# Softmax weights of the mixers scaled on ScalarE instead of VectorE, and tile 0's expert rows placed 3.45 apart in the written order of a one-core decoder layer

## The chip, the cores and the metric

One core of a Trainium2 chip runs the whole program. The metric is device time in microseconds (us), the median of three runs. TensorE is called PE below, VectorE DVE, ScalarE ACT, GpSimd POOL and SyncE SP, as the profile does. Everything is fp32, except where a projection splits its operands into a high and a low part.

## The reference, cut to what matters

1024 new prompt tokens and 64 sample tokens pass one decoder layer. Two mixers (a gated recurrence, "GLA", and windowed attention with a sink) read one input projection; their gated sum goes through an output projection; then a retrieval layer ("PEER") picks 128 of 16384 one-neuron experts for each token. The attention weights are what the change touches:

```
s = q . k * HD**-0.5, masked;  m = max(max_k s, sink)
e = exp(s - m);  p = e / (sum_k e + exp(sink - m));  o = p @ v        # 16 heads, 256 keys
```

and the expert layer is what fills most of the time:

```
act = gelu(x . u[idx_k]);  out = sum_k g_k * act_k * v[idx_k]         # k = 0..127 for each token
```

Each u row and v row is 4 KB. One gather brings one expert row for each of the 128 tokens of a tile, so 128 u gathers and 128 v gathers for a tile, 0.5 MB each.

## The kernel before, in words

Tokens come in 8 prompt tiles of 128 (0 to 7) and a tile of 64 sample tokens (8). The work before the experts goes in phases: projection of tiles 0 to 2, mixer of tile 0, feed group 0 (merge of the two branches, output projection, norm, queries and key scores for the experts of tile 0); then mixers of tiles 1 and 2 and feed group 1; then the projection of tiles 3 to 5, mixers 3 to 5 and feed group 2; then the projection of tiles 6 to 8, mixers 6 and 7, the samples' mixer and feed group 3. The expert layer of the tiles already scored runs beside this, and alone at the end.

The order of each engine's instructions is written out by a planner. Every piece of work is a generator (`mix_dve`, `mix_act`, `mix_pe`, `expert_dve`, ...) that yields the *place* of its next piece, a number of about a microsecond; `merged` takes, for each engine, always the piece with the smallest place. A place is no time: once the order is written, each engine runs its list strictly in order, and a piece waits for its semaphores with all that stands behind it. POOL has a list of its own without places: for each tile and head the u gathers, and from tile 1 on after each u gather one v gather of the tile before. The ring of u rows (L1881) holds 8 gathers, freed by the dot products, the ring of v rows (L1891) holds 8, freed by PE's sums.

Experts count in *slots*, one u row of one tile in each. Slot p has the place

```
at_slot(p) = start + p * SLOT_US + gaps at or before p
```

On DVE a slot is one dot product of 128 x 1024 (L2096) and, in 13 of a head's 16 slots, one step of the selection of the experts two heads ahead (L1970 to L2025). On PE the sums of tile t (L2180) stand from slot 128 (t + 1) on, the first one 5 slots later. On ACT, the gelu of tile t (L1923) stands at slot 128 (t + 1) + 0.2, followed by the copies that PE's sums need (L1926, L1935). A gap is put in so that the selection of a tile's first head does not stand ahead of its scores: slot 96 is at least 8 behind the scores of feed group 1, slot 352 at least 8 behind those of group 2.

The places that matter, worked out from the code (planner numbers, not measured times): `start` 393.6; mixer 1 from 423.1 and mixer 2 from 507.1 to 591.1; feed group 1 from 595.1 to 784.1 (its scores of head 1 at 732.1); slot 96 at 740.1 and slot 128 at 832.9; the projection of tiles 3 to 5 from 790.4 to 1037.4, its first product at 803.0; mixers 3 to 5 from 1045.4 to 1297.4; slot 352 at 1496.8.

Inside the mixer of tile t (`mix(t, x)`, x in steps of 1.05 places, for tile 0 1.3): DVE takes the attention scores from PSUM (L1173), ACT does the 16 exponentials with their sums (L1043) and `e_done`; the four recurrence heads go on beside it. Recurrence head h needs exponents (DVE, L1104), their exponentials (ACT, `gla_exp`, L1019 to L1022), `rescale` (DVE, L1114), scores (PE, L1234), `masked` (DVE, L1126), the output (PE, L1243, L1244), the copy `kpT` (ACT, L1049), the state update (PE, L1253) and `advance` (DVE, L1131). After x = 64 PE turns the scaled attention weights (L1293), ACT copies them (L1060), PE multiplies by the values (L1304). DVE's scaling stands at x = 48 to 51, between the exponents of head 3 and `masked` of head 2.

Of the kernel before, what the change touches and what calls it, by code (L numbers as in the profile page):

```python
# [23 lines left out]
ALU = mybir.AluOpType  # L24
ACT = mybir.ActivationFunctionType
AX_X = mybir.AxisListType.X

P = 128
# [14 lines left out]
SWA_HEADS, KV_HEADS, HD, WINDOW = 16, 2, 64, 128  # L43
# [124 lines left out]
MIX_PHASES = ((0,), (1, 2), (3, 4, 5), (6, 7))  # L168
FEEDS = len(FEED_TILES)
KEPT = FEEDS - 1  # L170
SLOT_US = 2.90
MIX_US = 80.0
SAMPLE_US = 150.0
KEYS = WINDOW + STEPS
# [5 lines left out]
def layer_stage(nc, sem, i_, o_, z_tok, z_feat, z_kv, z_kT, z_b, oa_rows, ob_cols, h_rows, xn_rows, scores):  # L180
# [6 lines left out]
    with ExitStack() as ctx:  # L187
# [148 lines left out]
        M, N_ = shared(mix_fill), shared(sample_fill)  # L336
# [47 lines left out]
        s_taken = sem("m_s_taken")  # L384
        neg_ready = sem("m_neg_ready")
        e_done = sem("m_e_done")
        p_ready = sem("m_p_ready")
        pT_ps = sem("m_pT_ps")
        pT_ready = sem("m_pT_ready")
# [141 lines left out]
        def mix(t, x):  # L531
            base, stretch = mix_at[t]
            return base + stretch * x
# [8 lines left out]
        start = scored(0, 1) + 26.0  # L542
        gaps = []

        def at_slot(p):
            return start + p * SLOT_US + sum(extra for first, extra in gaps if p >= first)

        for g in range(1, FEEDS):
            first = (FEED_TILES[g][0] * HEADS - 2) * TOPK
# [485 lines left out]
        def mix_act(act, t):  # L1035
# [9 lines left out]
            for h in range(GLA_HEADS):  # L1045
                yield mix(t, (34.5, 42.3, 53.5, 60.0)[h])
                act.wait_ge(sc_done, GLA_HEADS * t + h + 1)
                wait(act, su_done, GLA_HEADS * t + h - 1)
                act.activation(M.kpT[:, h % 2, :], X[:, BANK + h * P:BANK + (h + 1) * P], ACT.Copy).then_inc(kpT_ready, 1)  # L1049
                if h < 2:  # L1050
                    yield mix(t, exp_at(h + 2))
                    gla_exp(act, t, h + 2)
            yield mix(t, 62.5)
            norm_squares(act, M, t, P)
            yield mix(t, 65.0)
# [100 lines left out]
        def mix_dve(dve, chain, t):  # L1156
# [43 lines left out]
            yield mix(t, 48.0)  # L1200
            dve.wait_ge(e_done, t + 1)
            chain.link(dve.tensor_tensor(M.m[:, 3, :], M.e_sum[:, :], M.m[:, 2, :], ALU.add))
            chain.link(dve.reciprocal(M.m[:, 3, :], M.m[:, 3, :]))
            for q in range(4):
                if q:
                    yield mix(t, 48.0 + q)
                heads = slice(4 * q, 4 * q + 4)
                last = dve.tensor_tensor(M.s[:, heads, :], M.s[:, heads, :],
                                         M.m[:, 3, heads].unsqueeze(2).to_broadcast([P, 4, 2 * P]), ALU.mult)
                if q < 3:  # L1210
                    chain.step(last)
            last.then_inc(p_ready, 1)
            yield mix(t, 52.5)
            masked(dve, t, 2)
            yield mix(t, 53.5)
# [1084 lines left out]
```

## Time and profile before

| | |
|---|---|
| median of 3 runs | 4101.09 us (4090.44 to 4101.35) |
| the profiled execution | 4111.9 us, its span 4110.1 us |
| PE busy | 3062.5 us (75%) |
| DVE busy | 2435.0 us (59%) |
| POOL busy | 2350.9 us (57%) |
| ACT busy | 715.2 us (17%) |
| moved by DMA | 1450.92 MB, mean 353 GB/s |

Busy shares are means over stages with different limits; the stages have to be read one by one. "DMA share" is the mean busy share of the core's 16 DMA engines; it reads up to 1.03 or 1.04 where they are full.

### The profile page before, as it was taken

How to read it: one execution, taken by the hardware profiler on the slowest of the kernel's cores; microseconds unless marked ns; L12 is line 12 of the kernel's file. 1: busy time of each engine (PE TensorE's matmuls, PEld its weight loads, DVE VectorE, ACT ScalarE, POOL GpSimd, SP SyncE). 2: the span in 40 equal slices, each digit the busy share in tenths (PEclk: the TensorE clock that was granted, in tenths of full speed). 3: DMA queues.
4: the chain of work that ended last, by engine and by line, in shares of the span. 5: the costliest groups of instructions: out<-in, count | busy, mean ns of one | idle time of the engine just before them, and what ended most of it. 6: DMA issues, size and time to landing. Idle time of an engine off the chain costs nothing.

```text
span 4110.1 us, 40041 instructions
## 1 busy us (share of the span) xinstructions
PE 3062.5 (75%) x14004; PEld 1684.9 (41%) x14004; DVE 2435.0 (59%) x6237; ACT 715.2 (17%) x1573; POOL 2350.9 (57%) x2188
## 2 busy tenths in 40 slices
PE   8988458789957698979876767597965665665667
PEld 7887337677723345547753312244510000010111
DVE  3342885476677855467658857365566666665540
ACT  5461220243223200133222101000100000000000
POOL 0000332255667856466657757566677777777775
PEclk9999559899977799989987766798977777778999
DMA  4537768799999999899999999999999999999999
GB/s 151 165 121 279 252 227 299 243 345 414 413 337 349 344 409 411 334 393 410 414 395 347 366 357 393 380 368 412 412 401 409 409 409 407 409 407 373 397 409 351
DMA packets 451617, 1450.92 MB, mean 353 GB/s; under 512 B 52184, under 2 KB 135192, under 8 KB 431048
## 3 DMA queue, kind: packets, MB, share of 16 engines
q0 software_dynamic: 313344, 1140.99, 71.6%
q1 hardware_dynamic: 138072, 307.37, 20.6%
q8 instruction: 111, 1.82, 0.2%
q14 instruction: 90, 0.74, 0.0%
HBM read 1384.54 MB, written 64.82 MB: 353 GB/s over the span
## 4 chain that ended last, share of the span: by engine, by line
PE 33%; DMA 23%; POOL 21%; issue 10%; DVE 9%; ACT 2%; SPq 1%; POOLq 0%; DVEq 0%; ACTq 0%; PEldq 0%
DMA e_v_rows<-in_v,e_expT 16%; POOL e_v_rows L1891 11%; POOL e_u_rows L1881 10%; PE e_o_ps L2180 7%; PE O L1789 6%; PE X L1754 5%; DVE e_u_rows L2096 3%; PE X L1771 2%; PE e_o_ps L856 1%; PE e_o_ps L858 1%; PE e_o_ps L857 1%; PE X L856 1%; PE U L1805 1%; DMA f_obT<-ob_cols 1%; DMA f_ring<-in_w_feed 1%
## 5 line engine op out<-in xcount | busy, mean ns | idle before, releaser
L1881 POOL DMA_INDIRECT e_u_rows<-in_u,e_expert x1024 | 1119.4, 1093 | 1164.2 <-DVE e_dots L2096 511.8
L2180 PE MATMUL e_o_ps<-e_v_rows,e_zw 128*32 128x512 f32 x4352 | 1236.1, 760 | 580.1 <-DMA e_v_rows<-in_v,e_expT 567.9
L2096 DVE CUSTOM_DVE_ANT_0 e_u_rows<-e_u_rows,e_xn 128x1024 f32<-128x1024 f32 x1088 | 1326.1, 1220 | 533.6 <-DMA e_u_rows<-in_u,e_expert 408.4
L1891 POOL DMA_INDIRECT e_v_rows<-in_v,e_expT x1088 | 1166.9, 1073 | 558.1 <-issue 280.7
L2180 PEld LDWEIGHTS e_o_ps<-e_v_rows,e_zw 128*32 128x32 f32 x4352 | 205.5, 123 | 1481.6 <-DMA e_v_rows<-in_v,e_expT 1143.9
L1789 PE MATMUL O<-f_oaT,f_ring 128*128 128x384 f32 (+2 forms) x1024 | 264.7, 414 | 1.5 <-ACT f_oaT L1646 0.8
L810 DVE TENSOR_TENSOR jb_wl<-jb_w,jb_wh 128x512 fp32r<-128x512 f32 (+1 forms) x200 | 131.9, 688 | 183.6 <-ACT jb_wh L733 183.3
L1789 PEld LDWEIGHTS O<-f_oaT,f_ring 128*128 128x128 f32 x1024 | 176.2, 195 | 79.2 <-issue 13.1
L1754 PE MATMUL X<-f_oaT,f_ring 128*128 128x384 f32 (+2 forms) x512 | 138.8, 427 | 46.8 <-DMA f_ring<-in_w_feed 40.1
L733 ACT ACTIVATE jb_wh<-jb_w 128x512 fp32r<-128x512 f32 (+1 forms) x200 | 120.2, 628 | 156.1 <-PE X L858 77.0
L1754 PE MATMUL X<-f_obT,f_ring 128*128 128x384 f32 (+2 forms) x512 | 135.1, 419 | 15.3 <-DMA f_obT<-ob_cols 15.3
L1771 PE MATMUL X<-f_ring,f_mT 128*128 128x256 f32 x576 | 131.4, 386 | 7.9 <-DVE f_obT L1703 3.5
L856 PE MATMUL X<-jb_xh,jb_wh 128*128 128x384 f32 x360 | 127.0, 353 | 11.2 <-DVE jb_wl L810 11.0
L1754 PEld LDWEIGHTS X<-f_oaT,f_ring 128*128 128x128 f32 x512 | 90.5, 201 | 96.7 <-DMA f_ring<-in_w_feed 41.5
L1935 ACT ACTIVATE e_zw<-e_wT 128x32 f32<-128x32 f32 (+1 forms) x36 | 8.8, 249 | 696.8 <-PE e_o_ps L2180 696.5
L810 DVE TENSOR_TENSOR ja_wl<-ja_w,ja_wh 128x512 fp32r<-128x512 f32 (+1 forms) x100 | 67.4, 691 | 105.0 <-ACT ja_wh L733 104.7
L1771 PEld LDWEIGHTS X<-f_ring,f_mT 128*128 128x128 f32 x576 | 108.8, 192 | 36.0 <-issue 21.9
L857 PE MATMUL X<-jb_xl,jb_wh 128*128 128x384 f32 x360 | 122.5, 340 | 0.0
L858 PE MATMUL X<-jb_xh,jb_wl 128*128 128x384 f32 x360 | 122.4, 340 | 0.0
L1754 PEld LDWEIGHTS X<-f_obT,f_ring 128*128 128x128 f32 x512 | 89.9, 197 | 60.3 <-DMA f_obT<-ob_cols 16.2
L1234 PE MATMUL X<-qt,rel 128*128 128x16 f32 x512 | 90.7, 324 | 28.8 <-DVE kp L1121 28.8
L1234 PEld LDWEIGHTS X<-qt,rel 128*128 128x128 f32 x512 | 92.5, 274 | 41.3 <-issue 35.5
(315 smaller groups left out, 4527.6 us busy)
## 6 DMA issues: line engine op xcount, KB each, us to landing
f_ring<-in_w_feed SPq DMA_DIRECT2D x80, 1024.0 KB, 8.2
jb_w<-in_w_big SPq DMA_DIRECT2D x48, 1024.0 KB, 8.3
ja_w<-in_w_big SPq DMA_DIRECT2D x24, 1024.0 KB, 5.1
e_v_rows<-in_v,e_expT POOLq DMA_INDIRECT x1088, 9.9
e_u_rows<-in_u,e_expert POOLq DMA_INDIRECT x1024, 10.1
z_feat<-jb_stage SPq DMA_DIRECT2D x64, 192.0 KB, 7.6
e_sc<-scores SPq DMA_DIRECT2D x36, 256.0 KB, 6.9
z_feat<-ja_stage SPq DMA_DIRECT2D x32, 192.0 KB, 1.9
```

The lines of the kernel that those rows point to most:

```text
L810: dve.tensor_tensor(quarter(r.wl[q % 2], c, part), quarter(r.w[q % 2], c, part), quarter(r.wh, c, part).bitcast(F32), ALU.subtract).then_i ...
L856: pe.matmul(out, lhs[0][:, k, :], rhs[0][:, k, :], start=(k == 0), stop=False)
L857: pe.matmul(out, lhs[0][:, k, :], rhs[1][:, k, :], start=False, stop=False)
L858: last = pe.matmul(out, lhs[1][:, k, :], rhs[0][:, k, :], start=False, stop=(k == KT - 1))
L1234: pe.matmul(X[:, h * P + j * SUB:h * P + (j + 1) * SUB], M.rel[:, h % 2, j, :], M.qt[:, h % 2, j * SUB:(j + 1) * SUB], start=True, stop=True)
L1754: last = pe.matmul(w_ps[b][:, 0:size(g) * P], weight[:, k, :], src[:, k, 0:size(g) * P], start=(k == 0), stop=(k == KT - 1))
L1771: last = pe.matmul(w_ps[item % 2][:, 0:WIDTH], F.mT[:, k, i * P:(i + 1) * P], weight[:, k, :], start=(k == 0), stop=(k == KT - 1))
L1789: last = pe.matmul(q_ps[half][:, 0:size(g) * P], weight[:, k, half * P:(half + 1) * P], F.xnT[:, k, 0:size(g) * P], start=(k == 0), stop=( ...
L1881: pool.indirect_dma_start(u_ring[:, count % U_RING, :], None, u_dram, bass.IndirectOffsetOnAxis(ap=index, axis=0)).then_inc(u_got[count % ...
L1891: pool.indirect_dma_start(v_ring[:, count % V_RING, :], None, v_dram, bass.IndirectOffsetOnAxis(ap=expT[:, t % 2, n:n + 1], axis=0)).then_ ...
L2096: dve.tensor_tensor_reduce(u_ring[:, count % U_RING, :], u_ring[:, count % U_RING, :], xn[:, t % 2, :], 1.0, 0.0, ALU.mult, ALU.add, dots[ ...
L2180: last = pe.matmul(o_ps[32 * j:32 * (j + 1), cols], zw[:, part % 2, j, hot_col:hot_col + 32], v_ring[:, (first + j) % V_RING, cols], start ...
```

## The change

Two edits. First, the multiplication of the 16 heads' exponentials by the reciprocal of their sum goes from DVE (four instructions of four heads, L1204 to L1212) to ACT (16 instructions of one head, `Copy` with a scale per partition, in place). They stand at x = 51.0 to 52.5 on ACT, behind `gla_exp` of head 3 and ahead of the copy `kpT` of head 2. The first waits for the new semaphore `r_ready`, which DVE's reciprocal counts up; the last counts up `p_ready`, as DVE's last one did. DVE keeps the sum and the reciprocal. Second, the first 128 slots (tile 0's u rows) are placed 3.45 apart instead of 2.90; `gaps` is worked out by the same rule with the new places.

```diff
--- before.py
+++ after.py
@@ -168,7 +168,7 @@
 MIX_PHASES = ((0,), (1, 2), (3, 4, 5), (6, 7))
 FEEDS = len(FEED_TILES)
 KEPT = FEEDS - 1
-SLOT_US = 2.90
+SLOT_US, FIRST_US = 2.90, 3.45
 MIX_US = 80.0
 SAMPLE_US = 150.0
 KEYS = WINDOW + STEPS
@@ -384,6 +384,7 @@
         s_taken = sem("m_s_taken")
         neg_ready = sem("m_neg_ready")
         e_done = sem("m_e_done")
+        r_ready = sem("m_r_ready")
         p_ready = sem("m_p_ready")
         pT_ps = sem("m_pT_ps")
         pT_ready = sem("m_pT_ready")
@@ -543,7 +544,7 @@
         gaps = []
 
         def at_slot(p):
-            return start + p * SLOT_US + sum(extra for first, extra in gaps if p >= first)
+            return start + p * SLOT_US + min(p, P) * (FIRST_US - SLOT_US) + sum(extra for first, extra in gaps if p >= first)
 
         for g in range(1, FEEDS):
             first = (FEED_TILES[g][0] * HEADS - 2) * TOPK
@@ -1050,6 +1051,13 @@
                 if h < 2:
                     yield mix(t, exp_at(h + 2))
                     gla_exp(act, t, h + 2)
+                if h == 1:
+                    for k in range(SWA_HEADS):
+                        yield mix(t, 51.0 + 0.1 * k)
+                        if k == 0:
+                            act.wait_ge(r_ready, t + 1)
+                        scaled = act.activation(M.s[:, k, :], M.s[:, k, :], ACT.Copy, scale=M.m[:, 3, k:k + 1])
+                    scaled.then_inc(p_ready, 1)
             yield mix(t, 62.5)
             norm_squares(act, M, t, P)
             yield mix(t, 65.0)
@@ -1200,16 +1208,7 @@
             yield mix(t, 48.0)
             dve.wait_ge(e_done, t + 1)
             chain.link(dve.tensor_tensor(M.m[:, 3, :], M.e_sum[:, :], M.m[:, 2, :], ALU.add))
-            chain.link(dve.reciprocal(M.m[:, 3, :], M.m[:, 3, :]))
-            for q in range(4):
-                if q:
-                    yield mix(t, 48.0 + q)
-                heads = slice(4 * q, 4 * q + 4)
-                last = dve.tensor_tensor(M.s[:, heads, :], M.s[:, heads, :],
-                                         M.m[:, 3, heads].unsqueeze(2).to_broadcast([P, 4, 2 * P]), ALU.mult)
-                if q < 3:
-                    chain.step(last)
-            last.then_inc(p_ready, 1)
+            dve.reciprocal(M.m[:, 3, :], M.m[:, 3, :]).then_inc(r_ready, 1)
             yield mix(t, 52.5)
             masked(dve, t, 2)
             yield mix(t, 53.5)
```

## Rows read from the trace of the kernel before

**Rows 1.** The page: a DMA queue (packets, MB, share of 16 engines), a weight load

```profile
q0 software_dynamic: 313344, 1140.99, 71.6%
...
jb_w<-in_w_big SPq DMA_DIRECT2D x48, 1024.0 KB, 8.3
```

**Rows 2.** Stretches: busy us of PE, PEld, DVE, ACT, POOL; granted clock, DMA share, GB/s

```profile
250.00:270.00 20.00, 18.59 (x109) 17.43 (x108) 14.96 (x31) 11.16 (x19) 0.00 (x0) 1.00 0.33 112
...
440.00:600.00 160.00, 96.51 (x454) 68.08 (x450) 153.72 (x447) 50.17 (x147) 60.91 (x58) 0.58 0.65 202
600.00:690.00 90.00, 68.82 (x293) 57.44 (x294) 50.58 (x126) 0.37 (x1) 27.84 (x28) 0.89 0.93 353
690.00:750.00 60.00, 54.69 (x251) 46.06 (x251) 11.34 (x30) 9.86 (x23) 3.70 (x4) 0.93 0.55 194
...
800.00:870.00 70.00, 51.38 (x269) 47.11 (x269) 51.72 (x119) 31.60 (x55) 23.79 (x22) 0.79 0.80 298
870.00:1125.00 255.00, 235.39 (x1523) 192.85 (x1523) 167.29 (x377) 82.64 (x152) 151.71 (x140) 0.98 1.01 403
...
1155.00:1420.00 265.00, 190.43 (x966) 95.55 (x958) 227.28 (x656) 77.23 (x225) 204.11 (x163) 0.75 0.95 343
2150.00:2350.00 200.00, 138.86 (x634) 61.68 (x630) 169.36 (x494) 49.56 (x147) 152.19 (x126) 0.72 0.95 353
...
3000.00:3800.00 800.00, 493.27 (x1230) 74.44 (x1234) 512.83 (x1275) 18.89 (x36) 606.33 (x604) 0.77 1.02 404
```

**Rows 3.** Chain of waits from 438 to 600 us, its shares by line

```profile
by line: DVE e_u_rows L2096 29.1%; DVE s L1173 7.8%; DVE rel L1104 6.8%; DVE s L1208 5.7%; DVE rel L1114 4.2%; PE X L1234 4.0%; PE O L1243 3.8%; PE U L1253 3.7%; PE U L1304 3.0%; issue 2.9%; PE O L1244 2.6%; PE X L1293 2.3%; DVE S L1131 1.7
```

**Rows 4.** Groups of instructions, DVE, 440 to 600 us: count | busy, mean ns | idle

```profile
L2096 DVE CUSTOM_DVE_ANT_0 e_u_rows<-e_u_rows,e_xn 128x1024 f32<-128x1024 f32 x59 | 71.7, 1216 | 0.2 <-issue 0.2
```

**Rows 5.** Timeline of DVE: start, us, instruction; mixer 1

```profile
484.09 0.25 DVE L1203 RECIPROCAL m<-m 128x16 f32<-128x16 f32 x1
484.38 2.36 DVE L1208 TENSOR_TENSOR s<-s,m 128x1024 f32<-128x1024 f32 x2
...
488.40 2.35 DVE L1208 TENSOR_TENSOR s<-s,m 128x1024 f32<-128x1024 f32 x2
...
492.42 0.28 DVE L1126 TENSOR_TENSOR scm<-X,causal 128x128 f32<-128x128 f32 x1
```

**Rows 6.** Timeline of ACT, mixer 1

```profile
461.73 0.49 ACT L1043 ACTIVATE s<-s,m 128x256 f32<-128x256 f32 x1
462.12 0.19 ACT L1043 ACTIVATION_READ_ACCUMULATOR s<-s,m 128x1 f32 x1
...
484.43 0.25 ACT L1049 ACTIVATE kpT<-X 128x128 f32<-128x128 f32 x1
499.69 0.28 ACT L1049 ACTIVATE kpT<-X 128x128 f32<-128x128 f32 x1 [15.00 <-PE X L1236]
```

**Rows 7.** Timeline of PE, mixer 1

```profile
492.76 1.22 PE L1243 MATMUL O<-v,scm 128*128 128x256 f32 x2 [9.79 <-DVE scm L1126]
...
494.94 1.19 PE L1253 MATMUL U<-v,kpT 128*128 128x256 f32 x2
```

**Rows 8.** Timeline of DVE, slots between feed work

```profile
773.88 1.21 DVE L2096 CUSTOM_DVE_ANT_0 e_u_rows<-e_u_rows,e_xn 128x1024 f32<-128x1024 f32 x1
...
785.11 1.22 DVE L2096 CUSTOM_DVE_ANT_0 e_u_rows<-e_u_rows,e_xn 128x1024 f32<-128x1024 f32 x1
```

**Rows 9.** Waits from 597 to 800 us: in total, times, longest

```profile
DVE e_top_val L1970 <- DMA e_sc<-scores: 28.9, 1, 28.9
```

**Rows 10.** Timeline of PE, first product of the projection, first expert sum

```profile
815.69 0.56 PE L856 MATMUL X<-jb_wh,jb_xh 128*128 128x256 f32 x1
...
870.45 4.41 PE L2180 MATMUL e_o_ps<-e_v_rows,e_zw 128*32 128x512 f32 x32
```

**Rows 11.** Timeline of ACT, the copy that the first sum needs

```profile
858.23 0.26 ACT L1935 ACTIVATE e_zw<-e_wT 128x32 f32<-128x32 f32 x1
```

**Rows 12.** Timeline of POOL, the ninth v gather

```profile
873.40 0.94 POOL L1891 DMA_INDIRECT e_v_rows<-in_v,e_expT  x1 [22.43 <-PE e_o_ps L2180]
```


## Prediction

> **What bounds the kernel now.** I read the page first. The gathers of expert rows are 1140.99 of 1450.92 MB: 2176 gathers of 0.524 MB [rows 1], which is 1.28 us each at the 404 to 410 GB/s of the full stretches. Then a table by stretches [rows 2]. The reader is to see two kinds of stretch. From 870 us on the DMA share is 1.01, from 3000 to 3800 us 1.02 with PE and DVE at 62 and 64%: transfers set the pace, and work taken from DVE there is worth nothing in itself. From 440 to 600 us, while mixers 1 and 2 run beside tile 0's u rows, the DMA share is 0.65 and DVE is busy 153.7 of 160 us. There DVE sets the pace, and later time follows from it: feed group 1 can't begin before mixer 2 ends, DVE sits 28.9 us for feed group 1's scores [rows 9], and neither tile 1 nor the next projection begins before them.
>
> So I count in this way: the end moves by what is taken out of the stretches in which the DMA engines are not full. A shorter stretch that merely moves gathers into a full stretch gains nothing; gathers moved into 690 to 750 us, where the share is 0.55 [rows 2], cost nothing.
>
> The chain of waits of mixers 1 and 2 [rows 3] shows what DVE time is on the path: the dot products with 29.1% of 162 us, 47.1 us, the scaling with 5.7%, 9.2 us, which is all eight scalings of the two mixers (four each, 2.36 us the pair [rows 5]).
>
> **The change, part by part.**
>
> *DVE loses the scaling.* Each mixer's four instructions take about 4.7 us, between the reciprocal at 484.09 and `masked` of head 2 at 492.42 [rows 5], on which PE has waited 9.79 us [rows 7]. The reciprocal stays.
>
> *ACT gains 16 scalings.* No row shows Copy of 128 x 256 in SBUF with a scale per partition. The nearest is the exponential with a bias per partition on the same tile: 0.49 us, with the read of its sum starting 0.39 us behind its own start [rows 6]. The read falls away, so from one to the next the bounds are 0.39 and 0.49 us, 6.3 to 7.9 us for 16. I take 0.40, 6.4 us, because no accumulator is read. The cover is ACT's idle time: after the copy at 484.43 it waits 15.00 us for PE [rows 6]. `r_ready` comes at 484.3, just as `gla_exp` of head 3 ends (484.43), so its wait costs nearly nothing. What stands behind it on ACT is `kpT` of head 2. That copy moves from 484.4 to about 491.3, and PE's update needs it; PE's update stood at 494.94 [rows 7]. With the scaling gone from DVE, `masked` would come 4.7 us sooner, at 487.7, and the update at 489.9; now `kpT` holds it to about 491.7. So of 4.7 us the path gets 3.2. That is 6.4 us for mixers 1 and 2; the bounds are 3.4 (2 x 1.7, at 0.49 us each) and 9.2 (all of the row on the chain). The weights themselves are wanted only at x = 64, 12 us later. ACT.Copy (`kpT`) already stands between exponentials with no table load between, so none is added. The Trainium skill ("ScalarE: Activation LUTs", Rules for kernel authors) says to multiply on VectorE and not on ScalarE. Here the rule is right by the instruction (4.7 against 6.4 us) and silent on the cover; by it alone each of the eight tiles would lose 1.7 us.
>
> *Tile 0's mixer.* It runs beside the projection, with no experts. From 250 to 270 us PE is busy 18.6 of 20 us and ACT 11.2 [rows 2]. There the burst of 6.4 us delays ACT's copies of weights, which PE's products wait for; DVE's relief is worth little. Bounds 0 and +5, I take +2: ACT has 8.8 us free in these 20, but the burst comes in one piece.
>
> *Tile 0's slots wider.* Before, slot p stands at 393.6 + 2.90 p; mixers 1 and 2 cover 423.1 to 591.1, that is slots 10.2 to 68.1, 57.9 of them, and the trace has 59 dot products there [rows 4]. After, 393.6 + 3.45 p: slots 8.5 to 57.2, 48.7. So 9.2 slots leave this stretch. A slot costs DVE 1.60 us with its selection step: seven from 773.88 to 785.11 [rows 8]. That gives 14.7 us if DVE never idles; by the chain, 47.1 us over 59 dots is 0.80 us a slot, 7.4 us. DVE is busy 96% before, but with less of it PE's own chain (the turns at the end of each mixer) shows through, so I take 12.5, nearer to the upper. Together with the scaling, mixer 2 ends 19 us sooner (bounds 11 and 24). The 9.2 slots go to feed group 1, where DVE is busy 50.6 of 90 and then 11.3 of 60 us [rows 2]; all must be done before the scores come, and there were 28.9 us of nothing before that [rows 9]. Their gathers, 11.8 us of DMA, fit: the shares 0.93 and 0.55 leave some 6 + 28 us. So this costs 0; with no such room it would cost up to 11.8.
>
> *Tile 1's start.* The gap is worked out anew: slot 96 stands at 740.1 in both, but slots 96 to 128 are wider, so slot 128 moves from 832.9 to 850.5, +17.6, against the projection of tiles 3 to 5, whose places stay. All of tile 0's gelu, its weights and PE's first sum move behind 17.6 more places of projection. That matters: `e_zw` is ready at 858.2 [rows 11], but PE, in order, comes to the first sum at 870.45 [rows 10], and POOL has stood for 22.4 us with v's ring full [rows 12], at a DMA share of 0.80 from 800 to 870 us [rows 2]. From the first product (place 803.0, 815.69 us) to the first sum (place 847.4) PE took 54.8 us for 44.4 places, 1.23 us a place. After it is 62.0 places. The projection starts 17 us sooner (19 less the 2 of tile 0's mixer), at 798.7; with the same 1.23 the sum comes at 875.0, at 1.0 us a place at 860.7. DVE has 6.1 slots fewer before it, so I take 1.15: 870.0, the same moment as before. What is gained there is not the 17 us but only what the projection is ahead: 24 loads of 1.05 MB [rows 1] in 247 places are 0.10 MB a place, 1.8 MB in 17.6, 4.4 us at 408 GB/s, with the stores about 5. So of 17 us 5.5 survive: this part gives back 11.5 us, with bounds 2 (sum at 860.7) and 17 (sum at 875.0). After that the DMA share is 1.01 and it neither grows nor shrinks.
>
> *Slots 128 to 352* stand 17.6 later, those from 352 on 3.3 later (1500.1 against 1496.8; the second gap falls away). SP's score and row loads for the experts move with them; none has another's work waiting close behind that needs it sooner. In full stretches this is free; some 6 pairs are done after the projection instead of beside it. 0, bounds -3 and +5.
>
> *Mixers 3 to 7.* DMA shares of 0.95 and 0.95, DVE 86 and 85% busy [rows 2]. DMA idles about 0.08 x 265 and 0.08 x 200 us, 37 us in all. Five times 3.2 us of path is 16 us; as DMA is so near to full I take half, -8 (bounds 0 and -16).
>
> Sum: +2 - 19 + 11.5 + 0 - 8 = -13.5 us. The profiled execution, 4111.9 us with a span of 4110.1, would become 4098.4. It lies 10.8 us above the median of 4101.09, so I forecast 4101.1 - 13.5 = 4087.6, say 4088.
>
> **The rivals.**
>
> *The start of tile 1 is not held up.* If PE's first sum keeps its distance from the projection's start (its order costs nothing, because the projection itself runs freer), the 11.5 us stay: -25; with the scalings fully on the path and mixers 3 to 7 worth 16, -33: 4068. For it: DVE is relieved in just that stretch. Against it: `e_zw` was 12 us early, so it is PE's order that held, and that order gets worse.
>
> *It is all given back there.* The stretch gives 11 to 14 us, the first sum comes at 875, 17 us lost of the 19, and mixers 3 to 7 give nothing because DMA is full: about -2, 4099. For it: the DMA share of 0.95, the ring that stands full for 22.4 us already.
>
> *ScalarE's burst comes onto the path (slower).* In each mixer `kpT` of head 2 waits for 16 scalings. If they take 0.49 us and start late, because a dot product and a selection step (up to 1.8 us) stand ahead of the reciprocal, the path is 1.7 us longer per mixer instead of 3.2 shorter. That decides where `kpT` comes over 4.7 us behind DVE's `masked`. Then the scaling is worth +3.4 and +8.5 instead of -6.4 and -8, tile 0's mixer costs 5: -13.5 + 9.8 + 16.5 + 3 = +16, 4117. For it: the same order in seven mixers. Against it: ACT's 15 us of idle time and a start at 484.4. The skill's rule named above leads to this side; by its bare 1.7 us for eight tiles the change would be 13.6 us worse than without the move.
>
> **How the numbers follow.** Forecast 0.44 (own range 4078 to 4098), not held up 0.20, given back 0.24, slower 0.12. No change is here within 0.3%, 12.3 us, about what a measurement of this kernel can tell. Faster by more: 0.27 of the forecast's 0.44 and all of the 0.20, and 0.02 of the third: 0.49. Within: 0.17 + 0.20 + 0.03: 0.40. Slower: 0.02 + 0.09: 0.11. The range reaches from the second case's 4068 to below the slower one's: 4067 to 4110.
>
> **What would show it.** In the profile after: no DVE scaling; 16 ACT Copies of 0.4 us from one to the next, beginning under 1 us behind the reciprocal, no table load. Between mixer 1's exponents and mixer 2's last copy some 49 dot products instead of 59, and feed group 1's first product some 17 us sooner. DVE's wait for tile 1's scores shorter than 28.9 us. The projection's first product near 799, the first sum of PE still near 870, POOL's stand before it longer than 22.4 us. From 1155 to 1420 us the same stretch 4 to 5 us shorter. Wrong it would be, above all, if the first sum moved by as much as the projection, or if feed group 1 got longer because the gathers moved into it hold up its weights.

## The result and the profile after

The changed kernel takes 4061.23 us (median of 5 runs, 4051.83 to 4068.40), the kernel before 4101.35 us beside it (5 runs, 4090.44 to 4105.82): ratio 0.9913, 95% interval 0.9893 to 0.9932. A second set of six runs gave 0.9903 (0.9885 to 0.9922). So it is 35 to 40 us faster, not 13, and the time lies below the range. The profiled execution of it took 4060.05 us with a span of 4058.3.

The stretches of the profile after, same columns as [rows 2] (the second row ends with mixer 2's last product):

```profile
250.00:270.00 20.00, 16.51 (x91) 15.08 (x91) 7.91 (x20) 16.48 (x34) 0.00 (x0) 1.00 0.38 130
440.00:580.30 140.30, 94.98 (x448) 68.36 (x448) 127.14 (x390) 61.17 (x175) 51.98 (x48) 0.58 0.62 193
440.00:600.00 160.00, 99.46 (x460) 72.02 (x461) 131.07 (x398) 61.77 (x176) 56.28 (x52) 0.58 0.67 216
690.00:750.00 60.00, 53.28 (x249) 44.99 (x248) 29.34 (x77) 11.88 (x29) 19.17 (x17) 0.91 0.86 316
800.00:870.00 70.00, 60.98 (x355) 56.20 (x356) 53.91 (x132) 36.61 (x62) 22.30 (x23) 0.98 0.84 299
1155.00:1420.00 265.00, 194.06 (x1006) 95.19 (x1006) 204.03 (x614) 93.38 (x245) 196.42 (x168) 0.76 0.97 363
2150.00:2350.00 200.00, 135.47 (x652) 54.78 (x648) 140.56 (x409) 57.55 (x148) 148.74 (x126) 0.82 1.00 378
3000.00:3800.00 800.00, 500.81 (x1253) 75.77 (x1252) 504.76 (x1260) 17.56 (x35) 608.34 (x603) 0.77 1.02 403
```

From 440 to 600 us DVE is busy 131.07 us instead of 153.72, but the last 20 us of that stretch already belong to feed group 1. Up to mixer 2's last product it is busy 127.14 of 140.3 us, 91% instead of 96%: the bound of that stretch is loosened, not gone. From 690 to 750 us the share went from 0.55 to 0.86: the displaced gathers of tile 0, and all work there comes some 18 us sooner than before. The mixers' stretches have 0.97 and 1.00 where they had 0.95. The last one is as it was.

Mixer 1, the timelines of ACT, DVE and PE, to set beside [rows 5 to 7]:

```profile
478.83 6.49 ACT L1059 ACTIVATE s<-s,m 128x256 f32<-128x256 f32 x16 [0.56 <-DVE m L1211]
485.22 0.26 ACT L1050 ACTIVATE kpT<-X 128x128 f32<-128x128 f32 x1
```
```profile
478.54 0.25 DVE L1211 RECIPROCAL m<-m 128x16 f32<-128x16 f32 x1
...
480.14 0.27 DVE L1134 TENSOR_TENSOR scm<-X,causal 128x128 f32<-128x128 f32 x1
...
486.79 0.48 DVE L1139 SCALAR_TENSOR_TENSOR S<-S,eb,U 128x256 f32<-128x256 f32 x1 [3.09 <-PE U L1252]
```
```profile
480.46 1.22 PE L1242 MATMUL O<-v,scm 128*128 128x256 f32 x2 [3.93 <-DVE scm L1134]
...
485.53 1.22 PE L1252 MATMUL U<-v,kpT 128*128 128x256 f32 x2 [2.99 <-ACT kpT L1050]
```

The 16 scalings take 6.49 us, 0.40 from one to the next, 0.56 us behind the reciprocal, with no table load ahead of them. `masked` stands at 480.14, 1.35 us behind the reciprocal's end, but `kpT` comes only at 485.22. PE's update waits 2.99 us for it, and DVE's `advance` 3.09 us for the update. The burst is on the path of the mixer, and the chain of waits from 438 to 582 us says so too, with 8.2% for L1059 where DVE's scaling had 5.7% [rows 3]; the dot products fell from 29.1 to 23.1%. (The 9.4% of `f_ring` are one wait of 13.6 us that begins at 581.9, behind the mixers: feed group 1 stands for its weights, in the kernel before as well.)

```profile
by line: DVE e_u_rows L2095 23.1%; DMA f_ring<-in_w_feed 9.4%; DVE s L1181 8.8%; ACT s L1059 8.2%; PE X L1233 7.0%; DVE rel L1112 6.5%; PE U L1252 4.2%; DVE rel L1122 3.9%; issue 3.3%; PE U L1303 3.3%; PE O L1242 2.5%; PE X L1292 2.3%; DVE 
```

Four more readings: dot products from 440 to 600 us (59 in [rows 4]; 49 of the 51 lie ahead of mixer 2's last product, as predicted); DVE's wait for tile 1's scores (28.9 us in [rows 9]); PE's first product and first expert sum ([rows 10]); POOL's stand ahead of it ([rows 12]):

```profile
L2095 DVE CUSTOM_DVE_ANT_0 e_u_rows<-e_u_rows,e_xn 128x1024 f32<-128x1024 f32 x51 | 62.0, 1215 | 0.0
```
```profile
DVE e_top_val L1969 <- DMA e_sc<-scores: 20.5, 1, 20.5
```
```profile
795.91 0.56 PE L857 MATMUL X<-jb_wh,jb_xh 128*128 128x256 f32 x1
```
```profile
869.80 3.64 PE L2179 MATMUL e_o_ps<-e_v_rows,e_zw 128*32 128x512 f32 x32
```
```profile
871.98 0.94 POOL L1890 DMA_INDIRECT e_v_rows<-in_v,e_expT  x1 [22.01 <-PE e_o_ps L2179]
```

The projection begins 19.8 us sooner and the first sum comes at the same moment, 869.80 instead of 870.45, as worked out. What was not foreseen stands further on, at feed group 2. Kernel before, then after: PE's expert sums there, POOL's longest stand in that stretch, and the stretch from slot 352's dot product to slot 384's.

```profile
1645.76 1.47 PE L2180 MATMUL e_o_ps<-e_v_rows,e_zw 128*32 128x512 f32 x12
...
1677.59 1.92 PE L2180 MATMUL e_o_ps<-e_v_rows,e_zw 128*32 128x512 f32 x16
...
1691.85 1.92 PE L2180 MATMUL e_o_ps<-e_v_rows,e_zw 128*32 128x512 f32 x16
```
```profile
1679.77 0.93 POOL L1891 DMA_INDIRECT e_v_rows<-in_v,e_expT  x1 [22.23 <-PE e_o_ps L2180]
```
```profile
1646.70:1792.10 145.40, 123.43 (x536) 67.68 (x529) 63.59 (x158) 27.09 (x55) 75.92 (x71) 0.92 0.93 352
1117.50:1424.50 307.00, 208.59 (x1061) 101.57 (x1063) 245.27 (x712) 84.73 (x238) 222.16 (x181) 0.74 0.95 344
```
```profile
1635.26 1.92 PE L2179 MATMUL e_o_ps<-e_v_rows,e_zw 128*32 128x512 f32 x16
...
1650.18 1.92 PE L2179 MATMUL e_o_ps<-e_v_rows,e_zw 128*32 128x512 f32 x16
```
```profile
1652.36 0.97 POOL L1890 DMA_INDIRECT e_v_rows<-in_v,e_expT  x1 [5.18 <-PE e_o_ps L2179]
```
```profile
1631.50:1757.40 125.90, 105.44 (x485) 57.84 (x483) 64.03 (x156) 24.47 (x49) 71.45 (x72) 0.89 0.99 378
1093.60:1386.10 292.50, 199.93 (x1057) 96.24 (x1057) 228.84 (x701) 106.18 (x288) 207.58 (x177) 0.74 0.97 358
```

In the order before, the pause of 14.3 places ahead of slot 352 leaves PE 31.8 us between two batches of sums (1645.76 and 1677.59; the next follows after 14.3 us). v's ring stays full, POOL stands 22.23 us, the DMA share of the whole stretch is 0.93. After, the batches are 14.9 us apart, POOL's longest stand is 5.18 us and the share 0.99.

**A ledger.** All transfers are the same in both kernels, so I count idle DMA time: 1.03 times a stretch's length (1.03 is what the share reads where the engines are full), less the mean busy time of its DMA engines, between events that mean the same work. It was taken from two profiles of each kernel (g4_before_again and f4_control are the second ones).

| stretch ending at | before | after | difference | predicted |
|---|---|---|---|---|
| first expert sum of PE | 336.4, 334.0 | 324.7, 327.1 | -9.3 | -5.5 |
| last product of mixer 5 | 27.6, 25.1 | 19.9, 18.7 | -7.1 | -4.8 |
| slot 384's dot product | 16.4, 17.4 | 6.2, 6.8 | -10.4 | 0 |
| slot 640's dot product | 24.6, 24.4 | 13.4, 20.1 | -7.8 | -3.2 |
| end | 29.9, 29.8 | 27.2, 26.7 | -2.9 | 0 |

The sum is -37.5 us; the two spans differ by 44.6 on the mean (4110.1 and 4105.2 against 4058.3 and 4067.8), the rest is busy time of the DMA engines, which was 8 us less for the same bytes. Why it was less isn't shown. It was 3795 to 3800 us in the five profiles in which DVE scales in mixers 3 to 7 (before twice, e2, e4 and h1 below) and 3787 to 3797 in the thirteen others. (The predicted column splits -8 for mixers 3 to 7 as 3 to 2.) All five places gained more than foreseen, two of them had been put at nothing. Two profiles of one kernel differ by up to 2.5 us in a row, and by 6.7 at slot 640.

### The profile page after: what moved, and what is told of

Its sections match the earlier page's. It is cut to its first block, busy times and chain, and to the rows that moved or that the text cites. A ratio compares the mean times of both kernels' runs of the same rounds, so it can differ in the third digit from the quotient of the medians.

```text
span 4058.3 us, 40138 instructions
## 1 busy us (share of the span) xinstructions
PE 3052.4 (75%) x14004; PEld 1673.6 (41%) x14004; DVE 2399.8 (59%) x6205; ACT 768.3 (19%) x1702; POOL 2332.1 (57%) x2188
## 3 DMA queue, kind: packets, MB, share of 16 engines
q1 hardware_dynamic: 138072, 307.37, 20.9%
## 4 chain that ended last, share of the span: by engine, by line
PE 33%; DMA 26%; POOL 20%; issue 9%; DVE 9%; ACT 3%; SPq 1%; POOLq 0%; DVEq 0%; ACTq 0%; PEldq 0%
DMA e_v_rows<-in_v,e_expT 18%; POOL e_v_rows L1890 10%; POOL e_u_rows L1880 9%; PE e_o_ps L2179 7%; PE O L1788 6%; PE X L1753 4%; DVE e_u_rows L2095 3%; PE X L1770 2%; DMA jb_w<-in_w_big 1%; PE e_o_ps L857 1%; PE X L857 1%; PE e_o_ps L858 1%; PE e_o_ps L859 1%; PE X L859 1%; PE X L858 1%
## 5 line engine op out<-in xcount | busy, mean ns | idle before, releaser
L1880 POOL DMA_INDIRECT e_u_rows<-in_u,e_expert x1024 | 1106.1, 1080 | 1129.4 <-DVE e_dots L2095 478.1
L2179 PE MATMUL e_o_ps<-e_v_rows,e_zw 128*32 128x512 f32 x4352 | 1248.6, 754 | 577.4 <-DMA e_v_rows<-in_v,e_expT 563.5
L1753 PEld LDWEIGHTS X<-f_oaT,f_ring 128*128 128x128 f32 x512 | 90.0, 199 | 88.8 <-DMA f_ring<-in_w_feed 32.4
```

The costliest lines, as they stand in the source:

```text
L1753: last = pe.matmul(w_ps[b][:, 0:size(g) * P], weight[:, k, :], src[:, k, 0:size(g) * P], start=(k == 0), stop=(k == KT - 1))
L1880: pool.indirect_dma_start(u_ring[:, count % U_RING, :], None, u_dram, bass.IndirectOffsetOnAxis(ap=index, axis=0)).then_inc(u_got[count % ...
L2179: last = pe.matmul(o_ps[32 * j:32 * (j + 1), cols], zw[:, part % 2, j, hot_col:hot_col + 32], v_ring[:, (first + j) % V_RING, cols], start ...
```

## The experiments

Slots "wide" are 3.45 apart. Ratios are to the kernel before on the same chip, with 95% intervals; its medians there were 4102.69, 4097.42, 4104.95 and 4098.80 us.

| run | ScalarE scales | slots wide | slot 128 | slot 352 | median us (runs) | ratio |
|---|---|---|---|---|---|---|
| e1_act_only | all mixers | none | 832.9 | 1496.8 | 4082.76 (12) | 0.9951 (0.9932 to 0.9971) |
| e2_wide_only | none | 0 to 128 | 850.5 | 1500.1 | 4078.06 (8) | 0.9935 (0.9911 to 0.9960) |
| e3_wide96 | all | 0 to 96 | 832.9 | 1496.8 | 4080.98 (10) | 0.9941 (0.9917 to 0.9965) |
| e4_act_early | 0 to 2 | 0 to 128 | 850.5 | 1500.1 | 4077.94 (8) | 0.9938 (0.9913 to 0.9964) |
| f1_late128 | all | 96 to 128 | 850.5 | 1500.1 | 4073.54 (6) | 0.9941 (0.9922 to 0.9961) |
| f2_gap256 | all | 0 to 96 | 832.9 | 1496.8 | 4090.00 (12) | 0.9971 (0.9955 to 0.9988) |
| f3_kpt_first | all, later | 0 to 128 | 850.5 | 1500.1 | 4066.31 (6) | 0.9918 (0.9900 to 0.9936) |
| f4_control | all | 0 to 128 | 850.5 | 1500.1 | 4062.06 (6) | 0.9903 (0.9885 to 0.9922) |
| g1_gap128 | all | 0 to 128 | 862.5 | 1512.1 | 4074.13 (6) | 0.9933 (0.9909 to 0.9957) |
| g2_pause352 | all | 0 to 128 | 850.5 | 1514.4 | 4081.54 (6) | 0.9948 (0.9928 to 0.9969) |
| g3_act_late | 3 to 7 | 0 to 128 | 850.5 | 1500.1 | 4063.97 (5) | 0.9912 (0.9889 to 0.9935) |
| g4_before_again | none | none | 832.9 | 1496.8 | 4096.93 (12) | 0.9987 (0.9968 to 1.0005) |
| h1_later_only | none | none | 850.5 | 1500.1 | 4089.23 (12) | 0.9983 (0.9968 to 0.9997) |
| h2_later_act | all | none | 850.5 | 1500.1 | 4072.42 (11) | 0.9939 (0.9918 to 0.9960) |
| h3_best | 3 to 7, later | 0 to 128 | 850.5 | 1500.1 | 4069.07 (6) | 0.9929 (0.9905 to 0.9954) |
| h4_no_pause | all | 0 to 96 | 832.9 | 1482.5 | 4091.45 (12) | 0.9987 (0.9967 to 1.0006) |

### The change in halves

Theory A held that each mixer passes its whole saving on and that the six slots that move behind the projection fill an idle wait; theory B is the prediction's own sum. e1_act_only sets `FIRST_US` to 2.90; e2_wide_only keeps the wide slots and puts DVE's four scalings back; e3_wide96 widens only slots 0 to 96, so that slots 128 to 351 stay where they were and the second gap is back; e4_act_early lets mixers 3 to 7 scale on DVE.

```diff
 e3_wide96
-            return start + p * SLOT_US + min(p, P) * (FIRST_US - SLOT_US) + ...
+            return start + p * SLOT_US + min(p, 96) * (FIRST_US - SLOT_US) + ...
 e4_act_early
-                if h == 1:
+                if h == 1 and t < 3:
```

> The scaling on ACT, tile 0's slots at 2.90 as before. Theory A (each of mixers 1 to 7 passes the whole DVE time of its scaling, 4.5 us, on to the end): about -32 us, 4069. Theory B (as predicted: the path gets 3.2 us in mixers 1 and 2, half of it in 3 to 7, +2 in tile 0's mixer): about -12 us, 4089. Under A mixers 3 to 5 together are some 13 us shorter in the trace, under B 5.

> Scaling on DVE as before, tile 0's slots at 3.45. Theory A (the six slots moved back past the projection later fill DMA time that stands empty in feed group 2): -8 to -12 us, 4091. Theory B (as predicted, what the mixers gain is given back at tile 1's start): -1 us, 4100; mixer 2 ends about 12 us sooner in both.

> The changed kernel, but only slots 0 to 96 are 3.45 apart; 96 to 128 are 2.90 apart and the second gap is back, so slot 128 stands at 832.9 and everything later where it stood before. Theory A: slower than the changed kernel by about 10 us, near 4071, with PE's first sum some 15 us sooner and the DMA engines idle again in feed group 2. Theory B: the 11.5 us given back at tile 1's start are saved, about 4050.

> The changed kernel, but mixers 3 to 7 scale on DVE again (the first three on ACT), slots wide. Theory A: slower than the changed kernel by five times 4.5 us, 22 us, near 4083. Theory B: by 8 us, near 4069.

Each half alone is worth about 20 us or more, against my -12 for the scaling and -1 for the slots. e1 lies between A's 4069 and B's 4089. Its mark in the trace decides nothing: mixers 3 to 5 are 12.7 us shorter than in the first profile of the kernel before (A had 13) and 5.4 shorter than in the second (B had 5). e2 is 22 us under B's 4100 and 13 under A's 4091; e3, which by B should have beaten the changed kernel, is 20 slower than it, 10 more than A had. e4 and the changed kernel differ by 0.9938 against 0.9913 and 0.9903, 10 to 14 us for scaling in mixers 3 to 7 (B had 8, A 22). The places of e3 beside those of the changed kernel: mixer 2 ends alike (281.1 us behind mixer 0's end against 280.7 and 282.7), its first sum comes at 854.5 instead of 869.8. Idle DMA time from slot 352 to 384 is 13.7 us in e3 and 14.6 in e1, and 6.1 and 5.4 in e2 and e4, whose slot 352 has no pause ahead of it.

### Where the later slots gain

f1_late128 widens only slots 96 to 128; f2_gap256 is e3_wide96 with its second gap put ahead of slot 256; f4_control is the changed kernel.

```diff
 f1_late128
+            return start + p * SLOT_US + (min(max(p, 96), P) - 96) * (FIRST_US - SLOT_US) + ...
 f2_gap256
-                gaps.append((first, need))
+                gaps.append((256 if g == 2 else first, need))
```

> ScalarE does the scaling, slots 0 to 96 stay 2.90 apart, only slots 96 to 128 are 3.45 apart: slot 128 stands at 850.5 as in the changed kernel, there is no second gap, and mixers 1 and 2 keep all their dot products. Theory A (what tile 1's later slots are worth is the waiting time in feed group 2, which six slots more fill, and it does not depend on the early slots): 10 to 19 us below the 4082.8 of the scaling alone, 4064 to 4072, and the stretch from slot 352's dot product to the projection of tiles 6 to 8 loses some 9 us of idle DMA time. Theory B (later slots are worth nothing by themselves, and the 12 us or so that mixers 1 and 2 gain by fewer slots are what counts): 4083, or up to 5 us more.

> ScalarE does the scaling, only slots 0 to 96 are 3.45 apart, so slots 128 to 255 stand where they did before; the second gap of 14.3 is put ahead of slot 256 instead of slot 352, so slots 256 to 351 stand 14.3 later than in e3_wide96 and only five slots more fall into feed group 2's wait. Theory A (filling that wait is the gain of the later slots): 8 to 12 us below e3_wide96's 4081, about 4071, and idle DMA time between slot 352's dot product and the next projection falls from 13.6 to about 5 us. Theory C (the gain is at tile 1's start, where slot 128's gelu and PE's first sum stand later): as e3_wide96, 4081.

> The changed kernel itself, once more, on the same chip as the other three. If its 4061.2 was a fair median, 4058 to 4065 and a ratio of 0.991; if its five runs happened to be low, nearer to 4068 to 4072 and a ratio of 0.993, and then the later slots are worth less than the 19 us that the medians gave them.

The control bears the first result out. f2 filled the wait at feed group 2, from 13.7 to 7.8 us of idle time, and lost more elsewhere: the pause of 14.3 places now stands beside mixers 3 to 5, which had a DMA share of 0.97 in the changed kernel:

```profile
1631.40:1764.60 133.20, 112.20 (x479) 59.28 (x479) 63.77 (x156) 25.19 (x50) 79.34 (x72) 0.87 0.97 374
1097.00:1391.10 294.10, 201.22 (x1042) 96.82 (x1043) 223.43 (x685) 104.34 (x286) 202.35 (x169) 0.76 0.93 340
```

0.97 behind slot 352, and 0.93 beside the mixers, 29.5 us of idle time instead of 15.0 in e3. The median is 4090.00, above e3's 4080.98, where theory A had 4071 and C 4081. So theory A names the place rightly and its price wrongly: it isn't enough to send slots into a hole, they must come out of a stretch that stays full without them. f1 takes them from the projection and gains, in the trace: slot 384 comes 32.4 us sooner than before, against 20.2 in e1. But that trace is of the fastest of f1's six runs (4062.88). The median, 4073.54, lies just above A's range and 9 us below e1's; by the ratios (0.9941 against 0.9951) it is 4 us, within the noise.

g2_pause352 adds 14.3 to the places from slot 352 on, g1_gap128 adds 12 from slot 128 on, both in the changed kernel. h4_no_pause is e3_wide96 without the second gap, h1_later_only the kernel before with 17.6 added from slot 128 on, h2_later_act the same with ScalarE's scaling.

```diff
 g2_pause352 (changed kernel), g1_gap128 (12.0 and P), h1_later_only (before, 17.6 and P)
-            return ... + sum(extra for first, extra in gaps if p >= first)
+            return ... + sum(extra for first, extra in gaps if p >= first) + (14.3 if p >= 352 else 0.0)
 h4_no_pause (e3_wide96)
-            need = scored(g, 1) + 8.0 - at_slot(first)
+            need = scored(g, 1) + (8.0 if g != 2 else -20.0) - at_slot(first)
```

> The changed kernel with the second gap back: slots 352 and later 14.3 places later (slot 352 at 1514.4, before 1496.8), tile 1's start untouched. Theory H: by the pause itself POOL's rings fill and the DMA engines idle; the wait of feed group 2 has 8 to 12 us more of idle DMA time, and the time is 4069 to 4074. Rival (slots 352 on wait for the scores in any case, so a pause of 14 places ahead of them hides in that wait, and the later slots only leave fewer places of the projection behind): 4059 to 4065.

> e3_wide96 (only slots 0 to 96 wide, slot 128 at 832.9) with the second gap left out, so that slots 352 on stand at 1482.5 instead of 1496.8 and nothing is displaced. Theory D (the displacement of slots 128 to 351 fills the wait for tile 3's scores; the pause is only where the wait shows): DVE waits for the scores with the same 352 slots done, the idle DMA time there stays at 13 us or more, 4081 to 4095. Theory P (the pause itself is the cost): 4062 to 4070, idle DMA time there about 5 us.

The pause alone costs 15 to 19 us: 4081.54 against 4062.06, by the ratios 0.9948 against 0.9903, or against the 0.9912 of g3, which is the changed kernel to within a measurement and ran beside it. The rival, that it hides in the wait for the scores, is out; theory H has the place right (10.6 us more idle time there, 8 to 12 foreseen) and the time some 7 us too low. Its trace shows the same pattern as that of the kernel before, sums of PE 27.1 and 19.4 us apart, POOL standing, a share of 0.92:

```profile
1635.67 1.92 PE L2179 MATMUL e_o_ps<-e_v_rows,e_zw 128*32 128x512 f32 x16
...
1662.79 1.92 PE L2179 MATMUL e_o_ps<-e_v_rows,e_zw 128*32 128x512 f32 x16
...
1682.21 1.92 PE L2179 MATMUL e_o_ps<-e_v_rows,e_zw 128*32 128x512 f32 x16
```
```profile
1664.97 0.94 POOL L1890 DMA_INDIRECT e_v_rows<-in_v,e_expT  x1 [17.51 <-PE e_o_ps L2179]
...
1684.38 0.94 POOL L1890 DMA_INDIRECT e_v_rows<-in_v,e_expT  x1 [9.78 <-PE e_o_ps L2179]
```
```profile
1631.20:1765.40 134.20, 110.75 (x508) 62.64 (x507) 63.05 (x156) 24.91 (x51) 67.77 (x67) 0.90 0.92 341
```

But one can't just strike the pause out. h4 does so without moving anything else. DVE then waits 32.30 us for tile 3's scores, with the same 354 dot products done as in the kernel before, where it waited 28.10:

```profile
1650.79 0.49 DVE L1969 MAX8 e_top_val<-e_sc 128x8 f32<-128x128 f32 x2 [32.30 <-DMA e_sc<-scores]
```

Idle time up to the projection's first product fell to 8.8 us, but slot 384 now lies ahead of that projection, and from 20 us ahead of its dot product to 60 us behind it the DMA engines idle for 15 us (1.5 before, 3.7 in the changed kernel), and up to slot 640 for 41.7 us (24.6 before); 4091.45. Theory D's time holds and so does its wait, but not its reason, that the idle time stays in the same place. Pause and displacement belong together: it is the displacement that lets the pause go.

> The kernel before with one edit: 17.6 is added to the places of slots 128 and later (128 at 850.5, the second gap falls away, 352 at 1500.1); slots 0 to 127 stay 2.90 apart and VectorE scales. Theory H (what moves the time is that six slots leave the full projection for feed group 2's wait and that the pause ahead of slot 352 goes): the stretch from slot 352's dot product to slot 384's loses 9 us of idle DMA time, 4077 to 4087, ratio 0.995. Theory E (it needs the earlier end of mixer 2, since tile 1's start would otherwise come later): the first sum 15 us later, 4095 to 4105.

> The changed kernel, but with slots 0 to 127 at 2.90 and 17.6 added from slot 128 on: ScalarE's scaling and the later slots, no slot wider. Theory H: as the changed kernel within 8 us, 4062 to 4070, since fewer dot products beside mixers 1 and 2 only bring forward a feed group whose tile then waits for PE's first sum. Theory E: the wider slots of tile 0 are worth 10 us or more of their own; 4072 to 4080 (f1_late128, with a part of the slots wide, had 4073.5).

> The changed kernel with slots 128 and later another 12 places later (slot 128 at 862.5, slot 352 at 1512.1). Theory H (the end moves by idle DMA time alone: a slot that leaves a full stretch for one with idle DMA time gains, and the later start of tile 1 costs little, 3.6 us of idle time for the 17.6 places between e3_wide96 and the changed kernel): idle time before the first sum grows by 2 to 3 us, that of feed group 2's wait falls by the 4.8 us that are left at most, 4056 to 4063. Theory B (the prediction's: what tile 1's start is later is lost, some 0.65 us for a place): 8 us longer, 4069.

h1 shows the price at tile 1's start bare. The first sum comes 18.7 us later than before (889.15), and from the first product to the end of that sum's first product (815.3 to 889.8) the share is 0.76:

```profile
1657.30:1789.10 131.80, 110.97 (x509) 61.36 (x507) 63.73 (x158) 25.48 (x51) 80.64 (x77) 0.91 0.99 373
815.30:889.80 74.50, 66.07 (x387) 60.55 (x389) 52.83 (x124) 38.36 (x65) 22.57 (x21) 0.96 0.76 267
```

That is 20.3 us of idle time where the kernel before has 12.0 (0.82 of 55.8 us) and the changed one 16.0 and 14.6. So tile 1's later start costs 8 us with no cover and 3 to 4 us when mixer 2 ends early; against it stand 9.5 us less behind slot 352. By the medians h1 is 7 to 10 us below the kernel before, less than H said and more than E. With ScalarE scaling (h2) the wide slots are missed by 10 us in the medians and 11 to 15 by the ratios (0.9939 against 0.9913 and 0.9903), though by slot 384 they are worth only 7.6 to 10.8 of clock there, 3.4 of them from a longer first phase in h2's profile. This agrees with f1, and with E rather than H. g1 shows the other end: 12 places more cost 12 us (4074.13, 0.9933), more than either theory had; idle time before the first sum rises to 20.7 us as B had it, but 26.0 us stand in mixers 3 to 5 (16.6 and 15.1 in the changed kernel), where neither theory had looked. H fell there: its gain behind slot 352 (2.9 us left) did come.

### Is ScalarE's burst on the path?

f3_kpt_first moves the 16 scalings behind `kpT` of head 2 (x = 53.6); g3_act_late lets the mixers of tiles 0 to 2 scale on DVE; h3_best does both.

```diff
 f3_kpt_first
-                if h == 1:
+                if h == 2:
-                        yield mix(t, 51.0 + 0.1 * k)
+                        yield mix(t, 53.6 + 0.1 * k)
 g3_act_late
-                if h == 1:
+                if h == 1 and t >= 3:
```

> The changed kernel with the 16 scalings moved behind the copy kpT of head 2 on ScalarE (x = 53.6 instead of 51.0). Theory D (the burst is on the path of mixers 1 and 2, since kpT waits for it): the state update of head 2 comes some 3 to 5 us sooner in each mixer, mixer 2's last product 4 to 8 us sooner, and the time is 4 to 8 us below the changed kernel's 4061, 4053 to 4057. Rival: the burst then holds the exponentials or kpT of head 3 or the turned weights in the same way; 4061 within 3.

> The changed kernel, but in the mixers of tiles 0, 1 and 2 the scaling stays on VectorE. Theory H: with the wider slots VectorE is no longer full there, the two mixers are 2 to 4 us longer, and PE's first sum comes at the same 870 us as it does in every kernel whose slot 128 stands at 850.5; 4061 to 4066. Theory B (scaling in mixers 1 and 2 is worth 6.4 us, in tile 0's -2): 4065 to 4068, and mixer 2's end 6 us later.

> The changed kernel with two edits of the runs before together: mixers 0 to 2 scale on VectorE, and from mixer 3 on ScalarE's 16 scalings stand behind the copy kpT of head 2 (x = 53.6). If kpT's wait is on the path of mixers 3 to 7, where the DMA engines are not quite full, mixers 3 to 5 have 3 to 5 us less idle DMA time and the time is 4052 to 4060; if a mixer's time there is hidden by transfers, 4060 to 4066 as the changed kernel.

f3's update follows `masked`'s product without a stop, the scalings come later:

```profile
483.85 1.22 PE L1242 MATMUL O<-v,scm 128*128 128x256 f32 x2 [3.93 <-DVE scm L1134]
...
486.03 1.19 PE L1252 MATMUL U<-v,kpT 128*128 128x256 f32 x2
```
```profile
481.56 0.25 ACT L1050 ACTIVATE kpT<-X 128x128 f32<-128x128 f32 x1
482.21 6.49 ACT L1059 ACTIVATE s<-s,m 128x256 f32<-128x256 f32 x16 [0.40 <-DVE m L1211]
```

Mixers 1 and 2 took 274.9 us instead of 280.7 and 282.7, as theory D had it, and slot 384 came 9 to 12 us sooner than in the changed kernel. Yet the median is 4066.31 against 4062.06, no gain: D's 4053 to 4057 is out, and it lies above the rival's 4061 within 3 too. In the profile 8 us are lost behind slot 640 (1435.5 us from there to the end, 1427.6 in both profiles of the changed kernel), but at slot 640 it was 10 and 20 us ahead, and it is the fastest of its six executions (4057.76). So this trace doesn't show where the others lose the gain. g3 is the changed kernel to within a measurement (0.9912), and mixers 1 and 2 take 280.4 us in it: with the wide slots, who scales in mixers 1 and 2 makes no difference. h3 has no gain either: 4069.07 lies above both of its ranges, and mixers 3 to 5 have 16.9 us of idle time in it, as in the changed kernel. No version measured beats the changed kernel.

> The kernel before once more, for a second profile of it: 4097 to 4103, ratio 1.000. If the stand of PE between mixer 6's last product and mixer 7's first score (18.6 us in the first profile, in which expert sums wait for their v rows) is in the written order, it is here again; if it is chance, it need not be. The idle DMA time by stretch should repeat within 2 us up to slot 512 and may differ by 10 us at the start of feed group 3.

g4 repeats within 2.5 us in each stretch of the ledger, its median within the noise. PE's stand behind mixer 6 is there again, 15.2 us, so it is in the written order.

## Why the prediction was wrong

**Tile 0's mixer, +2.** Not told apart from 0: mixer 0 ends at 299.6 us in both, though from 250 to 270 us ACT is now busy 16.48 of 20 us. Over all profiles it ends between 297.1 and 303.5, on the mean at 298.9 with DVE scaling in it and at 300.5 with ScalarE.

**Mixers 1 and 2, -19.** Right as a sum: mixer 2's last product moved from 599.7 to 580.3. The split into 6.4 and 12.5 was not. The scaling alone (e1) gives 6.8 us there, the wide slots alone (e2) 17.1, both 19.4 and 17.4 in the two profiles (each counted from mixer 0's end). They take the same DVE time out of one stretch, and once one has loosened it, the other finds little. That `kpT` would hold the update back behind `masked` was foreseen, and was measured (2.99 us). But 18 us of clock were not 18 us of idle DMA time. Some ten dot products fewer were done by then (60 and 61 instead of 71 and 70), so the idle time of the mixers fell by 3 us only; the gathers went to feed group 1, whose idle time fell by 8.

**Tile 1's start, +11.5: somewhat mis-sized.** The event was right: the first sum stood at 869.8 where 870.0 was worked out, the projection's first product at 795.9 (798.7). In the prediction's own terms 5.5 us were to survive of the sooner start. Over two profiles of each kernel the projection starts 18.1 us sooner and 9.3 us of idle time are saved by the first sum (ledger), so 8.8 us were given back, not 11.5. What I had too small is the work that goes over while the first sum waits: from first product to first sum the share is 0.82 in both kernels, over 74.5 us instead of 55.8, and 21.4 MB were moved in it instead of 16.8, 3.1 MB more of weights and stores and 1.6 MB more of gathers. I had 1.8 MB of weights, with the stores 5 us. POOL's stand for v's ring didn't grow (22.01 us, 22.43 before), against what was foreseen. Counted from the projection's first product, idle time grew by 3 to 4 us; h1 and g1, with the start later against less cover, show 8 and 5 to 6.

**Slots 128 to 352, 0 with bounds -3 and +5: the step that failed.** I wrote that in full stretches the shift is free, and looked at no row of feed group 2. There the kernel before had a wait of 28.1 us of DVE for scores, 22.23 us of POOL, and a share of 0.93. That the second gap fell away was named in the prediction and priced at nothing. It is the largest single term: 10.4 us of idle time in place (ledger), and 15 to 19 us of time when the pause is put back (g2). Of these g2's profile has 10.6 in the same place and 4.3 more up to slot 640. The rest was not found in one place. One candidate is the order around mixer 7. Before and after, PE from mixer 6's last product to mixer 7's first score:

```profile
2247.87 0.67 PE L1304 MATMUL U<-pT,vv 128*64 128x128 f32 x8
...
2263.51 3.62 PE L2180 MATMUL e_o_ps<-e_v_rows,e_zw 128*32 128x512 f32 x10 [0.97 <-DMA e_v_rows<-in_v,e_expT]
2267.06 1.19 PE L1270 MATMUL X<-kk,sq 64*128 64x256 f32 x4
```
```profile
2206.05 1.42 PE L1303 MATMUL U<-pT,vv 128*64 128x128 f32 x16
...
2207.66 0.70 PE L1269 MATMUL X<-kk,sq 64*128 64x256 f32 x4
```

In the six profiles with slot 352 at 1496.8 or sooner (before twice, e1, e3, f2, h4) expert sums that wait for v rows stand between, 15 to 19 us; in the twelve with it at 1500.1 or later it is 0 to 1.3 us. So a shift of 3.3 places changed that order. What it is worth wasn't separated: e1 has the stand and reaches slot 640 as fast after slot 384 (875.1 us) as the changed kernel (873.3 and 879.5). Before (twice), e3 and f2 take 891 to 897, but so do g1 and g2, with 894 and no stand. Another candidate is the wait for loads at feed group 3 (last section): where it is 9 to 10 us, or none as in e1, slots 384 to 640 take 871 to 879 us (g1 alone 894), where it is 14 to 22, they take 879 to 912. What the further 5 to 9 us are stays open.

**Mixers 3 to 7, -8 with bounds 0 and -16: mis-sized.** e4 and the changed kernel give 10 to 14, within the bounds. The idle time fell in mixers 3 to 5 from 23.2 and 20.9 to 16.6 and 15.1 us, and stayed at 20.6 with DVE scaling (e4). Halving for a share near 0.95 was too timid: 12 us are three quarters of the 16 us of path, and half of the 23.5 us that DVE spent. How they arise is shown in part only: over the whole profile e4 has 2 us more idle DMA time than the changed kernel's two, and 10.5 us more busy time of the DMA engines.

**The rivals.** "Not held up", with 4068, came nearest in time and was wrong in its event: the first sum did not move. "All given back" and "ScalarE's burst" are out (two sums were off: +2 - 19 + 17 is 0, not -2, and "not held up" with all of its terms is 3 us lower, 4065); the latter's mechanism, `kpT` behind the burst, is real and cost nothing that the medians show (f3). The rule of the Trainium skill ("ScalarE: Activation LUTs", Rules for kernel authors) of multiplying on VectorE would have cost 10 to 14 us in mixers 3 to 7 here (e4), and nothing in mixers 1 and 2 once the slots are wide (g3); by the bare instructions it stays right, 6.49 against 4.7 us.

Summed by the ledger, in idle time, -9.3 - 7.1 - 10.4 - 7.8 - 2.9 = -37.5 against the predicted -13.5. Of the 24 us missed 10.4 stand at the pause, 3.8 ahead of the first sum, 2.3 in mixers 3 to 5, 4.6 from slot 384 to 640 and 2.9 behind; for the last two no cause was shown.

## What to carry to other kernels

Where transfers bound most of the time, make a ledger of idle DMA time by stretch before pricing a change of order, and ask of every moved piece which stretch it leaves and which it enters; from a full one into a hole it gains (f1, 12 us by slot 384 in its trace, 4 to 9 in its time), out of a nearly full one it makes a new hole (f2). A derived quantity of the order, here a gap that a rule makes or drops, is part of the change and deserves a price of its own: 14 places cost 15 to 19 us. Clock and idle time are two currencies: a stretch that ends sooner with fewer transfers done has gained less than its clock says. Two edits that relieve the same engine in one stretch don't add.

## What was not expected of the hardware

The executions of one kernel lie 5 to 37 us apart (4083 to 4118 for the kernel before in one set), and some of that is settled at one place. At the start of feed group 3 PE needs three loads of 0.5 MB that share full DMA engines with the gathers. In the three profiles below they land 18 to 43 us after their issue (19 to 38 in the first, 18 to 38 in the second, 33 to 43 in the third, f4_control). PE's wait there, in the kernel before and in two executions of the changed one:

```profile
2661.76 8.24 PE L1754 MATMUL X<-f_obT,f_ring 128*128 128x384 f32 x16 [15.29 <-DMA f_obT<-ob_cols]
```
```profile
2607.06 6.81 PE L1753 MATMUL X<-f_obT,f_ring 128*128 128x384 f32 x16 [9.68 <-DMA f_obT<-ob_cols]
```
```profile
2615.68 7.67 PE L1753 MATMUL X<-f_obT,f_ring 128*128 128x384 f32 x16 [19.21 <-DMA f_obT<-ob_cols]
```

The two profiles of the changed kernel, 4058.3 and 4067.8 us, are 3.1 us apart at slot 384, 0.6 at slot 512 and 9.4 at slot 640, behind this wait of 9.68 or 19.21 us. What makes the loads slower in one than in the other isn't shown. A difference below 10 us between two single profiles of this kernel is no evidence about an edit elsewhere.
